# Three VectorE additions moved to GpSimd in a two-layer hybrid decoder trunk

## The reference, cut to what matters

```python
def _modulate(c_act, w, b):
    m = (c_act @ w + b)[:, None, :]
    shift, scale, gate = jnp.split(m, 3, axis=-1)
    return shift, scale, gate

for l in range(DEPTH):
    shift, scale, gate = _modulate(c_act, w_ada[l, 0], b_ada[l, 0])
    h = _rms(x, norm_gain[l, 0]) * (1.0 + scale) + shift
    x = x + gate * _hybrid_mixer(h, positions, cos, sin, w_in[l], ...)
    shift, scale, gate = _modulate(c_act, w_ada[l, 1], b_ada[l, 1])
    h = _rms(x, norm_gain[l, 1]) * (1.0 + scale) + shift
    if l % 2 == 0:
        f = _swiglu(h, ffn_w_gate[j], ffn_w_up[j], ffn_w_down[j])
    else:
        f = _moe(h, w_router[j], moe_w_gate[j], moe_w_up[j], moe_w_down[j])
    x = x + gate * f
```

## Time and profile before

| | |
|---|---|
| median of 3 executions | 1435.79 us (1435.27 to 1437.94) |
| profiled execution, its own time | 1435.91 us |
| its span, first to last instruction | 1434.2 us |
| granted TensorE clock, mean | 0.999 |
| PE busy | 1398.1 us (97%), 6878 instructions |
| DVE busy | 1237.1 us (86%), 1088 |
| ACT busy | 898.7 us (63%), 792 |
| POOL busy | 45.2 us (3%), 79 |
| chain that ended last, by engine | PE 87%, DVE 6%, DMA 3%, ACT 2% |

### The profile page before, as it was taken

How to read it: one execution, slowest core, us unless ns; L and a number is a source line. 1 busy time by engine, 2 the same in 40 slices (tenths; PEclk the granted TensorE clock), 3 DMA queues, 4 the chain that set the end, 5 groups by cost and what they waited for, 6 DMA issues and landing times.

```text
span 1434.2 us, 18304 instructions
## 1 busy us (share of the span) xinstructions
PE 1398.1 (97%) x6878; PEld 1137.2 (79%) x6878; DVE 1237.1 (86%) x1088; ACT 898.7 (63%) x792; POOL 45.2 (3%) x79
## 2 busy tenths in 40 slices
PE   5989999999999999999999999999999999999999
PEld 2765899996875888888888888888888888888886
DVE  3689768776878899999999999899999999999997
ACT  2074534443274677777777777777777777777774
POOL 0000000000000000000000000000000000000012
PEclk9999999999999999999999999999999999999999
DMA  9966669868627899999999999999999999999995
GB/s 368 414 255 217 241 221 372 296 258 337 241 109 278 298 364 375 358 394 396 340 395 395 340 398 394 391 346 393 395 340 396 396 341 397 393 382 356 393 391 149
DMA packets 195824, 484.50 MB, mean 338 GB/s; under 512 B 8926, under 2 KB 31684, under 8 KB 191684
## 3 DMA queue, kind: packets, MB, share of 16 engines
q1 hardware_dynamic: 187056, 451.17, 83.9%
q0 software_dynamic: 6480, 32.52, 6.1%
q10 hardware_dynamic: 2244, 0.22, 0.1%
HBM read 473.40 MB, written 10.49 MB: 337 GB/s over the span
## 4 chain that ended last, share of the span: by engine, by line
PE 87%; DVE 6%; DMA 3%; ACT 2%; SPq 1%; issue 1%; DVEq 0%; ACTq 0%
PE ps L1053 21%; PE ps L1055 21%; PE ps L1054 21%; PE ps L713 3%; PE ps L903 2%; PE ps L904 2%; PE ps L905 2%; PE ps L869 2%; PE ps L1096 2%; DMA split<-in_w_in 2%; PE ps L706 1%; SPq L456 1%; PE ps L911 1%; DMA arena<-in_w_ada 1%; PE ps L913 1%; PE ps L912 1%
## 5 line engine op out<-in xcount | busy, mean ns | idle before, releaser
L1970 DVE TENSOR_TENSOR split_r<-arena,split_r 128x2048 fp32r<-128x2048 f32 x336 | 763.6, 2289 | 62.0 <-ACT split_r L1379 61.5
L1379 ACT ACTIVATE split_r<-arena 128x2048 fp32r<-128x2048 f32 x334 | 640.4, 1918 | 125.2 <-PE ps L1055 121.9
L1053 PE MATMUL ps<-split_r,tokens_r 128*128 128x512 f32 x1280 | 505.4, 395 | 0.0
L1055 PE MATMUL ps<-split_r,tokens_r 128*128 128x512 f32 x1280 | 499.3, 390 | 0.0
L1054 PE MATMUL ps<-split_r,tokens_r 128*128 128x512 f32 x1280 | 498.3, 389 | 0.0
L1055 PEld LDWEIGHTS ps<-split_r,tokens_r 128*128 128x128 f32 x1280 | 240.3, 188 | 51.1
L1054 PEld LDWEIGHTS ps<-split_r,tokens_r 128*128 128x128 f32 x1280 | 240.7, 188 | 48.1
L1053 PEld LDWEIGHTS ps<-split_r,tokens_r 128*128 128x128 f32 x1280 | 240.5, 188 | 47.8 <-DVE split_r L1970 0.4
L903 PE MATMUL ps<-tokens_r,split_r 128*128 128x256 f32 x352 | 98.9, 281 | 1.3 <-DVE hT_r L1818 1.0
L904 PE MATMUL ps<-hT_r,split_r 128*128 128x256 f32 x352 | 99.3, 282 | 0.0
L905 PE MATMUL ps<-tokens_r,split_r 128*128 128x256 f32 x352 | 98.6, 280 | 0.0
(11 more groups left out here) (355 smaller groups left out, 1314.6 us busy)
## 6 DMA issues: line engine op xcount, KB each, us to landing
arena<-in_moe_w_gate SPq DMA_DIRECT2D x57, 2048.0 KB, 10.6
arena<-in_moe_w_up SPq DMA_DIRECT2D x57, 2048.0 KB, 10.9
arena<-in_moe_w_down SPq DMA_DIRECT2D x56, 2048.0 KB, 10.3
arena<-in_w_ada SPq DMA_DIRECT2D x15, 1024.0 KB, 20.1
arena<-in_w_ada POOLq DMA_DIRECT2D x10, 1536.0 KB, 10.3
arena<-in_ffn_w_gate SPq DMA_DIRECT2D x11, 1024.0 KB, 5.6
arena<-in_ffn_w_up SPq DMA_DIRECT2D x11, 1024.0 KB, 13.2
arena<-in_ffn_w_down SPq DMA_DIRECT2D x11, 1024.0 KB, 14.9
```

The lines of the kernel that those rows point to most:

```text
L1053: mm(out_, xh, h, start=first, stop=False, skip_group_check=True)
L1055: return mm(out_, xl, h, start=False, stop=last_, skip_group_check=True)
L1379: A(wh[:, j % SPLITS, :], piece_half(j), ACT.Copy).then_inc(sem("w_hi"), 1)
L1970: v.tensor_tensor(wl[:, j % SPLITS, :], piece_half(j), wh[:, j % SPLITS, :].bitcast(F32), ALU.subtract).then_inc(sem("w_lo"), 1)
```

## The change

Three additions or subtractions leave VectorE's stream and are put into GpSimd's: the low half of the first weight tile of the feed-forward (before the `bias` entry of the list `late`), the addition of the experts' gate bias row, and the low half of the first weight tile of the experts (both behind the DMA of that bias row). GpSimd waits for the same counters as VectorE did and raises the same ones. VectorE waits for the first low half to be counted before it makes its next one, so that the counts keep their order.

```diff
@@ GpSimd, layer 0, the list of late DMAs
                     for kind, a, k, cell, waits in late:
+                        if kind == "bias":
+                            pool.wait_ge(sem("f_hi"), 1)
+                            g.tensor_tensor(wl[:, 0, :], unit("g", 0), wh[:, 0, :].bitcast(F32), ALU.subtract)\
+                                .then_inc(sem("f_lo"), 1)
                         for name, value in waits:
                             pool.wait_ge(sem(name), value)
@@ GpSimd, layer 1
             pool.wait_ge(sem("ada_red"), 4)
             g.dma_start(moe_gate_bias, b_ada[1, 1, 2 * D:].unsqueeze(0)).then_inc(sem("late_bias_in"), 16)
+            pool.wait_ge(sem("late_bias_in"), 32)
+            g.tensor_tensor(moe_gate_acc[0:1, :], moe_gate_acc[0:1, :], moe_gate_bias, ALU.add)\
+                .then_inc(sem("gate_ok"), 1)
+            pool.wait_ge(sem("w_hi"), 1)
+            g.tensor_tensor(wl[:, 0, :], piece_half(0), wh[:, 0, :].bitcast(F32), ALU.subtract)\
+                .then_inc(sem("w_lo"), 1)
             pool.wait_ge(sem("hnat_ps"), 2)
@@ VectorE, end of the mixer
-                if l == 1:
-                    dve.wait_ge(sem("late_bias_in"), 32)
-                    v.tensor_tensor(moe_gate_acc[0:1, :], moe_gate_acc[0:1, :], moe_gate_bias, ALU.add)\
-                        .then_inc(sem("gate_ok"), 1)
                 dve.wait_ge(sem("rss_ps"), l + 1)
                 rstd(NT, 1.0 / LRU, 4, ps[:, 3, 0:NT])
                 assert rec_ms[l] == roots[0]
                 update(0, 0, 1, rs[:, 4:5])
-                if l == 1:
-                    low(0, 0)
-                else:
-                    dve.wait_ge(sem("f_hi"), 1)
-                    v.tensor_tensor(wl[:, 0, :], unit("g", 0), wh[:, 0, :].bitcast(F32), ALU.subtract)\
-                        .then_inc(sem("f_lo"), 1)
                 update(0, 1, 1, rs[:, 4:5])
@@ VectorE, dense, before its first low half
                 low_tokens(1)
+                dve.wait_ge(sem("f_lo"), 1)
                 low(1)
@@ VectorE, experts, before its first low half
+                dve.wait_ge(sem("w_lo"), 1)
                 low(0, 1)
```

## The result

The changed kernel takes 1440.68 us (median of 9 executions, 1438.79 to 1442.72). The kernel before, on the same chip and in the same rounds, takes 1437.11 us (9 executions, 1435.27 to 1437.94); its first three, which stood ahead of the prediction, had come out low at 1435.79. The ratio is 1.0027, interval 1.0019 to 1.0036: slower by 0.27%, 3.6 us between the medians (3.7 between the means). I had forecast +3.1 us and 1438.9 us. The time lies 0.3 us above my range.

The account below looks back on a forecast made before the run. The prediction took matrix products to bound the long loops, with VectorE late at layer 0's change and TensorE at layer 1's. Terms 2.1 + 1.1 + 0 = +3.2 us on 1435.91 gave 1439.1, forecast as 1438.9 us, range 1434.8 to 1440.4.

Parts of the forecast that it names:

- Prices on GpSimd: GpSimd's time, from memset and select rows: 4.8 us for a 2048-column subtraction, 2.5 us for the bias row.
- The standstill in layer 0: Layer 0: VectorE's first two-SBUF-input addition waits until GpSimd's subtraction ends, making the transposes late: +2.1 us.
- rival A: No standstill on either side, GpSimd's work wholly hidden: layer 0 gains 1.1 us, 1434.7 us; chance 0.10.
- The bias row: Layer 1: GpSimd's bias addition holds VectorE's 128x4 scaling 1.6 us; less 0.47 us slack, TensorE is late by +1.1 us.
- Layer 1's low half: End of layer 1's mixer: VectorE's addition may be held, yet is ready 0.1 us before TensorE's third group: 0.
- Rival D: Layer 0: the standstill leaves TensorE idle 3.1 us and its clock falls, 1.5 us more: 1440.4 us; chance 0.06.
- The base: Time of the kernel before that the forecast was added to: profiled execution 1435.91 us, median 1435.79 us.
- Does what is lost before a loop go through to the end?: Feed-forward and experts loops: a microsecond won or lost before one goes through to the end, only moving its start.

Follow-up runs that it names:

- e5: Changed kernel with GpSimd's layer-0 subtraction replaced by a memset of 3072 columns, which only writes; 1435.68 us, ratio 0.9993.
- e2: Kernel before with only the bias row and the experts' first low half moved to GpSimd; 1436.79 us, ratio 1.0006.
- e4: Changed kernel plus six unused products on TensorE ahead of the layer-0 transposes, filling its wait; 1437.97 us, ratio 1.0012.
- e9: Changed kernel with GpSimd's layer-0 subtraction cut into two instructions of 1024 columns; 1440.11 us, ratio 1.0023.

## Why the prediction was wrong

**Prices on GpSimd**: right, a little high. 4.53 us for the subtraction (forecast 4.8) and 2.34 us for the bias row (2.5). The GPSIMD Engine Reference's 4497 ns (the Trainium skill, section Performance versus the Vector engine) was nearer than my row of selects.

**The standstill in layer 0**: right, mechanism and place. Forecast +2.1 us, measured +1.66; GpSimd's 4.53 us in place of 4.8 account for 0.3 of the difference. e5 shows that the reading causes it, and rival A's 1.1 us gain was real where it is absent.

**The bias row**: mechanism right, size wrong, +1.1 against +0.33. The scaling was held 1.08 us instead of 1.6, as GpSimd began 1.94 us behind the DMA's issue instead of 2.2 and took 2.34 us instead of 2.5, and the slack behind it was 0.74 us instead of 0.47. I had read TensorE's idle time at the value products as the slack; e2 and the changed kernel give 1.40-0.66 and 1.08-0.33.

**Layer 1's low half**: right, 0, by 0.42 us (forecast 0.1). The 0.5 us that I gave for a GpSimd time of 6.1 us would be nearer 0.9 by the same rows; nothing here hung on it.

**Rival D is the step that failed.** The sum has no term for the clock; it was put at nothing, with a chance of 0.06, by the sentence that "it decides only where GpSimd takes more than 5 us". GpSimd took 4.53 us, TensorE was idle for 2.61 us, not 3.1, and the clock still fell: the row sums and transposes behind it took 1.63 us more, and e4, with the wait filled, took 1.64 us less. The threshold was taken from one row with a 3.59 us wait, which only showed that such a wait is enough, never that a shorter one isn't. The price that I worked out (+1.5) was right, the chance wasn't. It is also not the rule of all executions: e9's profile has the wait without the fall.

**The base** was the other 1.3 us. The three executions gave 1435.79; nine gave 1437.11. From 1437.11 my +3.1 would have given 1440.2, inside the range. That the forecast of the difference is only 0.5 us off the measured +3.6 is luck in part, as its errors offset: standstill -0.44, bias row -0.8, clock +1.6. Put right, the sum is 1.66+0.33+1.63 = 3.6 us. That it meets the medians' difference so closely is partly chance, since the last term isn't in every execution.

**Does what is lost before a loop go through to the end?** As far as the scatter lets one see. The feed-forward's stretch took 199.2 to 199.9 us in all profiles, with and without a late start.

## What to carry to other kernels

Before moving work to GpSimd, look at what VectorE does beside it: an addition with both inputs in SBUF stood until the end of a GpSimd instruction that reads SBUF, a small scaling with one input did too, and GpSimd's work cut in two, back to back, didn't free it. When a wait of TensorE grows, price the lower clock behind it from the rows that follow, not only the wait. And where an effect of 2 us in 1437 is argued, three executions of the base are not enough, and the mean clock doesn't tell which falls cost time: look at where the clock fell in more than one profile.

## What the runs showed of the hardware that I had not expected

- The granted clock fell to 0.50 after a wait of 2.61 us and, near 350 us, after one of 1.68 us in some executions; near 475 us, after one of 0.95 us, in two profiles; after 2.75 us in e9's profile it did not. The length of the wait alone doesn't decide.
- A 128x4 TENSOR_SCALAR, one input, is held as well: 1.25 and 1.57 us beside GpSimd's addition of the bias row, 0.17 without.
- A held addition ends some 0.56 us after GpSimd (4.72, 2.06 and 4.86 us beside 4.53, 1.90 and 4.67), so a short GpSimd instruction costs it its rest and no more.
